# Sparse attention's inputs: the compression's position as a further column, its halves in turn, and the gates in feature rows

## The reference, cut to what matters

```python
gates = jax.nn.sigmoid(proj[..., HD + 6 * KV_WIDTH_2:].reshape(B, S, H, 3))   # 48 columns
n_cmp = (S - CMP_LEN) // CMP_STRIDE + 1                                        # 31
blk_idx = np.arange(n_cmp)[:, None] * CMP_STRIDE + np.arange(CMP_LEN)[None, :]

def compress(t, pe, w1, w2):
    blocks = t[:, blk_idx] + pe[:, None, :]
    blocks = blocks.transpose(0, 1, 3, 2, 4).reshape(B, n_cmp, G, CMP_LEN * dh)
    return jax.nn.gelu(blocks @ w1) @ w2

kc = rotary(compress(k_cmp, pe_k, k_w1, k_w2), cmp_end_np, ROT_DIM, ROPE_THETA_2)
vc = compress(v_cmp, pe_v, v_w1, v_w2)
...
o = gb[..., 0:1] * o_cmp + gb[..., 1:2] * o_slc + gb[..., 2:3] * o_win
```

## Time and profile before

| what | value |
|---|---|
| median of 3 runs | 3114.63 us (3114.48 to 3114.65) |
| the profiled execution | 3115.59 us |
| its span in the trace | 3113.8 us |
| PE busy | 2821.1 us, 91% |
| DVE, ACT, POOL busy | 37%, 25%, 4% |
| mean granted TensorE clock | 0.951 |
| chain that ended last | PE 71%, DMA 13%, DVE 10%, ACT 4% |
| mean DMA rate | 193 GB/s |

### The profile page before, as it was taken

One profiled execution on the slowest core, in us unless ns is written; L12 is line 12 of the kernel. 1 busy time (PEld: TensorE's weight loads), 2 busy tenths in 40 slices (PEclk: granted clock), 3 DMA queues, 4 the chain that ended last, 5 costly groups with the idle time before them and its releaser, 6 DMA issues.

```text
span 3113.8 us, 32442 instructions
## 1 busy us (share of the span) xinstructions
PE 2821.1 (91%) x13640; PEld 1824.4 (59%) x13640; DVE 1142.1 (37%) x1674; ACT 782.5 (25%) x1220; POOL 122.6 (4%) x117
## 2 busy tenths in 40 slices
PE   6978799898889969989888999999999999999998
PEld 4534443333358544333337766878889865577886
DVE  4454521111153351111126644323341488433333
ACT  2342311000032121110014313222231365332222
POOL 1300100000000110000001000000010000000000
PEclk9998799999989979999999999999997799999999
DMA  8960389999933059999992203231340300032320
GB/s 295 335 228 15 135 334 428 428 413 426 427 115 114 15 208 407 427 416 425 426 376 87 77 32 109 73 116 57 119 114 2 82 1 1 15 127 81 108 88 34
DMA packets 125329, 601.03 MB, mean 193 GB/s; under 512 B 7184, under 2 KB 12560, under 8 KB 100352
## 3 DMA queue, kind: packets, MB, share of 16 engines
q1 hardware_dynamic: 120128, 584.27, 47.4%
q0 software_dynamic: 5056, 14.69, 1.5%
HBM read 596.84 MB, written 2.10 MB: 192 GB/s over the span
## 4 chain that ended last, share of the span: by engine, by line
PE 71%; DMA 13%; DVE 10%; ACT 4%; issue 1%; DVEq 0%; POOL 0%; SPq 0%; ACTq 0%; POOLq 0%
PE psum L285 69%; DMA weight_ring<-in_w_exp_down 7%; DVE scratch L235 4%; ACT scratch L273 4%; DMA scratch<-in_w_exp_down 3%; PE psum L300 3%; DMA weight_ring<-in_w_exp_up 2%; DVE scratch L3305 1%; DMA weight_ring<-in_w_exp_gate 1%; DVE scratch L268 1%; DMA weight_ring<-in_w_mix_in 1%; DVE scratch L1340 1%; DVE scratch L248 1%; DVE scratch L1701 0%; DVE scratch L1699 0%
## 5 line engine op out<-in xcount | busy, mean ns | idle before, releaser
L285 PE MATMUL psum<-scratch,scratch 128*128 128x512 f32 (+11 forms) x9072 | 1839.6, 400 | 90.7 <-ACT scratch L273 24.9
L285 PEld LDWEIGHTS psum<-scratch,scratch 128*128 128x128 f32 (+3 forms) x9072 | 1370.3, 188 | 555.6 <-issue 212.6
L285 PE MATMUL psum<-weight_ring,scratch 128*64 128x512 f32 (+2 forms) x3104 | 778.1, 610 | 95.9 <-DMA weight_ring<-in_w_exp_down 38.8
L285 PEld LDWEIGHTS psum<-weight_ring,scratch 128*64 128x64 f32 (+2 forms) x3104 | 264.1, 144 | 554.0 <-issue 455.4
L273 ACT ACTIVATE scratch<-psum 128x512 f32<-128x512 f32 (+5 forms) x332 | 192.8, 581 | 1074.5 <-PE psum L300 571.9
L235 DVE TENSOR_TENSOR scratch<-weight_ring,scratch 128x2048 fp32r<-128x2048 f32 (+2 forms) x110 | 241.9, 2199 | 517.6 <-ACT scratch L273 516.2
L273 ACT ACTIVATE scratch<-weight_ring 128x2048 fp32r<-128x2048 f32 (+2 forms) x110 | 202.5, 1841 | 580.5 <-PE psum L285 558.2
L235 DVE TENSOR_TENSOR scratch<-scratch,psum 128x512 f32<-128x512 f32 x92 | 63.3, 688 | 526.0 <-PE psum L285 524.5
L235 DVE TENSOR_TENSOR scratch<-scratch,scratch 128x512 fp32r<-128x512 f32 (+12 forms) x358 | 210.5, 588 | 63.5 <-ACT scratch L273 51.1
L273 ACT ACTIVATE scratch<-psum,scratch 128x128 f32<-128x128 f32 (+6 forms) x338 | 179.4, 531 | 182.8 <-PE psum L300 57.4
L300 PE MATMUL psum<-consts,scratch 128*128 128x128 f32 (+1 forms) x1016 | 162.3, 301 | 66.8 <-DVE scratch L235 47.7
(11 more groups left out here) (103 smaller groups left out, 642.4 us busy)
## 6 DMA issues: line engine op xcount, KB each, us to landing
weight_ring<-in_w_exp_gate SPq DMA_DIRECT2D x50, 2048.0 KB, 15.8
weight_ring<-in_w_exp_up SPq DMA_DIRECT2D x44, 2048.0 KB, 15.8
weight_ring<-in_w_exp_down SPq DMA_DIRECT2D x44, 2048.0 KB, 14.2
weight_ring<-in_ffn_w SPq DMA_DIRECT2D x28, 2048.0 KB, 7.8
weight_ring<-in_w_mod SPq DMA_DIRECT2D x24, 2048.0 KB, 9.8
scratch<-in_w_exp_up SPq DMA_DIRECT2D x20, 2048.0 KB, 15.8
scratch<-in_w_exp_down SPq DMA_DIRECT2D x20, 2048.0 KB, 14.2
scratch<-in_w_exp_gate SPq DMA_DIRECT2D x14, 2048.0 KB, 15.8
```

The lines of the kernel that those rows point to most:

```text
L285: ins = T.eng.matmul(out, lhsT, rhs, start=start, stop=stop)
```

## The change

The position's columns are loaded behind the 512 tokens of each group in `cmp_in` (now 544 long, in memory that starts where `vs` and `vw` start and reaches beyond them), and each of the first layer's products streams 33 columns for each group instead of 31: 31 blocks, one column that isn't used, and the position. The separate products for the position go. The loop over the halves moves inside the loop over l. The gates are made with the 48 gate columns as the stationary operand and x streamed, 512 tokens at a time; ACT takes one sigmoid over 48 partitions, PE transposes it in four pieces, and ACT copies the result to `gates`. `gatesT` lies in the first of the eight buffers of the turnings, so ACT waits for the turning of s.

```diff
@@ __init__
-        self.vs, self.vw = k.arena(NT, 256), k.arena(NT, 256)
+        at = k.arena.at
+        self.cmp_in = [k.arena(2, S + 32) for _ in range(2)]
+        self.vs, self.vw = k.arena.place(at, (NT, 256)), k.arena.place(at + 2 * S, (NT, 256))
...
-        self.cmp_in = [v.rearrange("p t n -> p (t n)").rearrange("p (g s) -> p g s", g=2) for v in (self.vs, self.vw)]
-        self.w2, self.pe_ = [k.arena(DH) for _ in range(2)], [k.arena(32) for _ in range(2)]
+        self.w2 = [k.arena(DH) for _ in range(2)]
+        self.gatesT = self.tm[0:48, 0, :]
@@ pool
-                          (self.w2[i][q], d[f"cmp_{n}_w2_2"]), (self.pe_[i][q], d[f"cmp_pe_{n}_2_T"])]
+                          (self.w2[i][q], d[f"cmp_{n}_w2_2"]),
+                          *[(self.cmp_in[i][q, g, S:S + 32], d[f"cmp_pe_{n}_2_T"]) for g in range(2)]]
@@ pe
-        token_pe(k, T, self.units["g"], [tile_parts(self.x, t) for t in range(NT)], lambda t: ("nsa", "g", t), 48, NC)
+        self.gates_pe(T)
         self.turned_pe(T, "w")
+        T.wait_ge(*k.at("nsa gates"))
+        bank = k.psum.take(T, ("nsa g turned",))
+        for t in range(NT):
+            tr(T, k, bank[:, t * 48:(t + 1) * 48], self.gatesT[:, t * P:(t + 1) * P], *([("full", "nsa g turned")] if t == NT - 1 else []))
         T.end(self.KEY)
+
+    def gates_pe(self, T):
+        k, u = self.k, self.units["g"]
+        bank = k.psum.take(T, ("nsa", "g"))
+        for i in range(2):
+            hi, lo = u.ready(T, i)
+            for c in range(4):
+                names = [("unit used", u.n0 + i)] if c == 3 else []
+                if i and c == 3:
+                    names.append(("full", "nsa", "g"))
+                mm3(T, bank[0:48, :], (hi[:, c, :], lo[:, c, :]), [x[:, 4 * i + c, :] for x in self.x], not (i or c), i == 1 and c == 3, *names)
@@ compress_up_pe
-        bank = k.psum.take(T, ("cmp pe", i))
-        for p in range(2):
-            q = slice(64 * p, 64 * p + 64)
-            for l in range(32):
-                mm(T, bank[q, 0:1], self.w1[i][q, l, :], self.pe_[i][q, l:l + 1], l == 0, l == 31,
-                   *([("full", "cmp pe", i)] if p and l == 31 else []))
-        for j in range(4):
+        for j in (2 * i, 2 * i + 1):
             T.wait_ge(*k.at("free", "nsa", "cmp", j))
         bank = k.psum.take(T, ("cmp up", i))
-        for p in range(2):
-            q = slice(64 * p, 64 * p + 64)
-            for l in range(32):
-                mm(T, bank[q, 0:2 * N_CMP], self.w1[i][q, l, :], src[q, :, l:l + 16 * (N_CMP - 1) + 1:16], l == 0, l == 31,
+        for l in range(32):
+            for p in range(2):
+                q = slice(64 * p, 64 * p + 64)
+                mm(T, bank[q, 0:2 * (N_CMP + 2)], self.w1[i][q, l, :], src[q, :, l:l + S + 1:16], l == 0, l == 31,
                    *([("full", "cmp up", i)] if p and l == 31 else []))
+    def compressed(self, i):
+        return self.k.psum.of(("cmp up", i))[:, 0:2 * (N_CMP + 2)].rearrange("p (g n) -> p g n", g=2)
@@ act
-            A.wait_ge(*k.at("full", "cmp up", i))
-            A.wait_ge(*k.at("free", "cmp pe", i))
+            A.wait_ge(*k.at("cmp bias", i))
...
-        for t in range(NT):
-            A.wait_ge(*k.at("full", "nsa", "g", t))
-            act(A, self.gates[:, t, :], k.psum.of(("nsa", "g", t))[:, 0:48], ACT.Sigmoid, ("free", "nsa", "g", t))
+        A.wait_ge(*k.at("full", "nsa", "g"))
+        for t in range(NT):
+            A.wait_ge(*k.at("full", "nsa", "s", "turned", t))
+        act(A, self.gatesT, k.psum.of(("nsa", "g"))[0:48, :], ACT.Sigmoid, ("free", "nsa", "g"), ("nsa gates",))
+        A.wait_ge(*k.at("full", "nsa g turned"))
+        act(A, self.gates, k.psum.of(("nsa g turned",))[:, 0:NT * 48].rearrange("p (t n) -> p t n", t=NT), ACT.Copy,
+            ("free", "nsa g turned"))
@@ dve
-            V.wait_ge(*k.at("full", "cmp pe", i))
-            copy(V, self.bias[:, i:i + 1], k.psum.of(("cmp pe", i))[:, 0:1], ("free", "cmp pe", i))
+            V.wait_ge(*k.at("full", "cmp up", i))
+            copy(V, self.bias[:, i:i + 1], self.compressed(i)[:, 0, N_CMP + 1:N_CMP + 2], ("cmp bias", i))
```

More of the change, by code:

```diff
@@ L2946, in act @@
         for i in range(2):
-            A.wait_ge(*k.at("full", "cmp up", i))
-            A.wait_ge(*k.at("free", "cmp pe", i))
+            A.wait_ge(*k.at("cmp bias", i))
             A.wait_ge(*k.at("nsa g zero"))
-            act(A, self.g_sb[:, i, 0:2 * N_CMP], k.psum.of(("cmp up", i))[:, 0:2 * N_CMP], ACT.Gelu_apprx_tanh, ("free", "cmp up", i),
-                bias=self.bias[:, i:i + 1])
+            act(A, self.g_sb[:, i, 0:2 * N_CMP].rearrange("p (g n) -> p g n", g=2), self.compressed(i)[:, :, 0:N_CMP],
+                ACT.Gelu_apprx_tanh, ("free", "cmp up", i), bias=self.bias[:, i:i + 1])
         u["s"].hi(A, 0)
@@ L2970, in cmp_copy @@
         lane.wait_ge(*k.at("full", "nsa", "cmp", j))
-        evac(lane, self.cmp_in[j // 2][:, j % 2, :], k.psum.of(("nsa", "cmp", j)), ("free", "nsa", "cmp", j))
+        evac(lane, self.cmp_in[j // 2][:, j % 2, 0:S], k.psum.of(("nsa", "cmp", j)), ("free", "nsa", "cmp", j))
     def copies(self, A, name):
```

## The result

The changed kernel takes 3058.27 us (median of 4 runs, 3057.05 to 3063.65) against 3114.56 us (4 runs) before: ratio 0.983, 95% interval 0.9816 to 0.9843. A second set of runs, on another occasion, gave 3058.99 against 3113.33 us, ratio 0.9829 (0.9815 to 0.9844). The forecast was 3059.4 us, range 3053 to 3069. The profiled execution took 3063.65 us, span 3061.6 us.

A forecast was written before the change was run, and what follows sets the result against it. The prediction took PE (TensorE, busy 91% of the span) to bound the kernel. Savings of 41.6 + 1.3 + 11.8 + 0.5 = 55.2 us took the median of 3114.63 us to 3059.4 us, range 3053 to 3069.

The forecast's parts named there:

- What bounds the stage: Sparse attention's input stage: PE holds the chain of waits, so shortening PE shortens the kernel until another engine is late.
- The position's products: Compression: 256 records leave; two more columns in each other product cost at most 0.007 us a record.
- The halves in turn: Compression: alternating halves run side by side at 0.058 us a pair, 7.4 us instead of 49.0, 41.6 us less.
- rival 3: Compression: halves take turns because their writes conflict in one bank; 14.3 to 28.9 us, 3066 to 3082 total; chance 0.05.
- One bank for two row tiles: Compression: the skill's rule forbids simultaneous use, giving 14.3 us at full clock; the forecast expected halves side by side.
- The clock under the pairs: Compression: clock stays at 1.00, so q1 also saves 1.3 us; the clock falling instead had chance 0.15.
- POOL's further loads: Ahead of the compression: four more position DMAs land at about 2317 to 2325, before PE asks at 2328.5; cost 0.
- The gates: Between q1 and attention: 24 products of 512 columns replace 96 of 48; 20.3 us becomes 8.5, 11.8 us less.
- The stall of s: After q1: PE's 1.6 us wait for the vector engine's split of s moves along and stays.
- The attention's start: First attention scores start at full clock and the vector engine's fill ends last; 0.5 us less.
- rival 2: Attention's start stays at full clock, giving 3055 to 3056 us in all; chance 0.15.
- The total: Whole kernel: 55.2 us less, giving 3059.4 us against the earlier median of 3114.63 us.

The follow-up runs named there:

- The kernel with blocks: The changed kernel with all 32 products of one half, then all 32 of the other, instead of alternating halves; median 3069.6 us (4 runs), ratio 0.9862.

## Why the prediction was right, and which term was off

- **What bounds the stage: right.** PE holds the chain through it before and after, and what was taken from PE there came off.
- **The position's products (counted within 49.0 to 7.4): right in kind.** The kernel with blocks has only this part of the compression's edit: 72.2 to 51.6 us, 20.6 us less.
- **The halves in turn: right that they run side by side, wrong in the price.** "I take 0.058" a pair should have been 0.115; 7.4 us became 14.7. The step that failed is the scaling of the earlier trace rows's 64x512 record by its columns. That record streams neighbouring columns, the compression's streams them 16 words apart. Such a record takes 0.107 us at half clock and 0.109 us at full. The earlier trace rows show records with stepped columns only at clock 0.50, and I read their 0.106 us as the price of the half clock; it was also the price of the step. At half clock the trace of before couldn't tell: there 62 stepped columns (first row) and a single column (second row) both take about 0.10 us a record.

```profile
2338.30:2351.50 13.20, 13.20 (x136) 13.20 (x136) 0.16 (x1) 1.28 (x1) 0.00 (x0) 0.50 0.00 1
2351.50:2364.20 12.70, 12.70 (x131) 12.70 (x129) 0.00 (x0) 0.31 (x1) 0.00 (x0) 0.50 0.00 1
```

  The 41.6 us was 34.3 (49.0 - 14.7). None of the rivals names the step. The size alone would have pointed to rival 3 (14.3 us), whose mechanism is refuted: the two records of a pair start within 9 ns of each other, and 7.6 us for all 256 records in one bank with neighbouring columns leaves no room for turns.
- **One bank for two row tiles: no cost here.** Halves on disjoint partitions of one bank accumulated side by side at 0.060 us a pair. The Trainium skill ("PSUM — Partial Sum Buffer", section "PSUM bank collisions raise a hardware error") quotes a rule against two row tiles in one bank without that exception; the traces disagree with it for this form. Further down the section reports the error for two row tiles in one bank and one quadrant of 32 partitions. These halves write different quadrants, so the traces agree with that narrower form as far as they go.
- **The clock under the pairs: right.** PEclk 1.00 over 14.7 us, q1 22.1 us. It fell under one half at a time with stepped columns and not under neighbouring ones (one trace each).
- **POOL's further loads: right at 0.** PE had no idle time ahead of the compression, and v's four loads landed after 6.6 us in the median, where its two had taken 9.6:

```profile
scratch<-in_cmp_pe_v_T POOLq DMA_DIRECT2D x4, 8.0 KB, 6.6
```

- **The gates: right.** 71.5 to 59.7 us, 11.8 forecast. The stall of s moved along unchanged (1.6 us), as forecast.
- **The attention's start: not met, and small.** The first scores were to run at full clock, with VectorE's fill ending last, 0.5 us less. In one trace of the changed kernel the clock fell 0.5 us behind the first score, and scores and fill end together; in the other it was 0.50 from the first score, and VectorE again waits 0.48 us for PE. The whole attention went from 195.6 to 195.4 and 194.3 us; the clock fell again, so rival 2 did not come.
- **The total: right by two errors that cancel, so by luck.** The stage gave 72.2 - 36.7 + 71.5 - 59.7 = 47.3 us and not 54.7. The two sets of medians moved 56.3 and 54.3 us. The 7 to 9 us more lie outside the stage, in instructions that the change leaves alone: some 3.8 us ahead of it, 0.2 to 1.4 us in the attention, and in some traces 3 us behind it (445.8 us in all of before, 445.7 and 442.6 in the two of the changed kernel). These 3 us are the clock's. All 14 traces take either 445.7 to 445.9 or 442.5 to 442.6 us there. The longer ones have two short falls to 0.50 on the way, 6.8 us in all (in the trace of before at 2735.3 and 3045.9); the shorter ones have neither. The shorter time came in 6 of the 10 traces with the changed compression and in none of the 4 with the old one. Whether the change causes this, say by where it puts the later work in time, or whether it is the spread of few runs, stays open.

## What to carry to other kernels

Price a small product by a record with the same step between its columns, and at the clock that it will run at: a rate seen only at half clock can hide a limit that shows at full clock. For f32 products like these (64x64 by 66 columns), put the columns that one product streams next to each other, or at most two words apart; if the tokens are wanted 16 apart, let the copy out of PSUM sort them, which cost nothing here. 64x64 products on the two diagonal quarters of the array run side by side even into one bank, and for the gates a few long streams beat many short ones twice, by their number and by the clock, which stayed up under them and fell under the short ones.

## What the runs showed of the hardware that was not expected

- A streamed f32 operand with a step of 4 or 16 words took 0.121 and 0.115 us a pair of 66 columns, with a step of 1 or 2 words 0.060 and 0.063 us, all at clock 1.00. A lone record with stepped columns costs 0.107 us at clock 0.50 and 0.109 us at 1.00.
- The clock stayed at 1.00 under lone 64x64 records with neighbouring columns (14.4 us), and fell after 3.9 us under the same records with stepped columns (one trace each).
- In the changed kernel records of the two halves of the array start within 9 ns of each other although both write the same bank, with different partitions.
- VectorE read PSUM with a step of 16 words in 0.69 us for 128x512, as fast as without; ScalarE read it in 0.60 us either way.
